# Stick-breaking loop on one core: the order of ScalarE's sigmoids and copies

## The reference

```python
z = einsum('bhtd,bshd->bhts', qb, k) * scale          # scores of a block of 128 queries
mask = s_pos[None, :] < t[:, None]
log_1m = where(mask, log_sigmoid(-z), 0.0)
log_a = log_sigmoid(z) + cumsum(log_1m, axis=3, reverse=True) - log_1m
a = where(mask, exp(log_a), 0.0)
out = einsum('bhts,bshd->bthd', a, v)
```

## Time and profile before

| what | value |
|---|---|
| median of three runs | 2631.31 us (2630.29 to 2631.83) |
| the profiled execution's own time | 2629.57 us |
| its span, first to last instruction | 2627.8 us |
| TensorE busy (all matmuls) | 2556.5 us, 97% |
| VectorE, ScalarE, GpSimd busy | 62%, 45%, 14% |
| the loop of the 40 tiles | about 854 to 945 us of the span |

### The profile page before, as it was taken

One profiled execution on the slowest core, in us unless ns is written; L12 is line 12 of the kernel. 1 busy time (PEld: TensorE's weight loads), 2 busy tenths in 40 slices (PEclk: granted clock), 3 DMA queues, 4 the chain that ended last, 5 costly groups with the idle time before them and its releaser, 6 DMA issues.

```text
span 2627.8 us, 38306 instructions
## 1 busy us (share of the span) xinstructions
PE 2556.5 (97%) x13432; PEld 2156.4 (82%) x13432; DVE 1621.5 (62%) x2801; ACT 1182.2 (45%) x1819; POOL 359.9 (14%) x322
## 2 busy tenths in 40 slices
PE   8999999999999899999999999999999999999997
PEld 6899978888888577888878878888879998788886
DVE  6588667664253647667346667664385885766733
ACT  4367554443232845444235554443343774544421
POOL 1011121110010522111010021110010111211100
PEclk9999999999999999999999999999999999999999
DMA  4410023332233012332322123333233001233231
GB/s 159 137 33 2 25 81 104 96 96 96 83 107 97 9 57 88 97 96 80 112 78 73 33 83 102 96 96 96 87 112 111 17 2 49 82 97 97 93 104 49
DMA packets 61908, 210.91 MB, mean 80 GB/s; under 512 B 8528, under 2 KB 10320, under 8 KB 61776
## 3 DMA queue, kind: packets, MB, share of 16 engines
q1 hardware_dynamic: 61776, 209.13, 25.1%
HBM read 207.01 MB, written 2.10 MB: 80 GB/s over the span
## 4 chain that ended last, share of the span: by engine, by line
PE 90%; DVE 7%; ACT 2%; issue 1%; POOL 0%; DMA 0%; SPq 0%; DVEq 0%; ACTq 0%; POOLq 0%
PE psum L304 21%; PE psum L305 21%; PE psum L306 21%; PE psum L1076 6%; PE psum L1064 3%; PE psum L905 3%; PE psum L907 3%; PE psum L906 3%; PE psum L1054 2%; PE psum L1053 2%; DVE xl L477 2%; DVE h L494 1%; PE psum L338 1%; DVE dh L493 1%; PE psum L332 1%
## 5 line engine op out<-in xcount | busy, mean ns | idle before, releaser
L304 PE MATMUL psum<-xh,w_hi 128*128 128x512 f32 x1712 | 667.0, 390 | 0.1
L305 PE MATMUL psum<-xh,w_lo 128*128 128x512 f32 x1712 | 666.1, 389 | 0.0
L306 PE MATMUL psum<-xl,w_hi 128*128 128x512 f32 x1712 | 666.1, 389 | 0.0
L266 DVE TENSOR_TENSOR w_lo<-w_raw,w_hi 128x1024 fp32r<-128x1024 f32 x226 | 280.2, 1251 | 513.4 <-ACT w_hi L260 511.4
L260 ACT ACTIVATE w_hi<-w_raw 128x1024 fp32r<-128x1024 f32 x226 | 236.1, 1057 | 564.8 <-PE psum L306 455.1
L304 PEld LDWEIGHTS psum<-xh,w_hi 128*128 128x128 f32 x1712 | 321.4, 188 | 66.9 <-issue 0.6
L306 PEld LDWEIGHTS psum<-xl,w_hi 128*128 128x128 f32 x1712 | 321.4, 188 | 66.7
L305 PEld LDWEIGHTS psum<-xh,w_lo 128*128 128x128 f32 x1712 | 321.5, 188 | 66.1
L698 DVE TENSOR_TENSOR w_lo<-w_raw,w_hi 128x1024 fp32r<-128x1024 f32 x160 | 209.3, 1308 | 253.7 <-ACT w_hi L694 253.7
L694 ACT ACTIVATE w_hi<-w_raw 128x1024 fp32r<-128x1024 f32 x160 | 168.4, 1053 | 234.7 <-PE psum L306 234.7
L304 PE MATMUL psum<-ah,w_hi 128*128 (+1 forms) x704 | 273.9, 389 | 0.0
(11 more groups left out here) (197 smaller groups left out, 3849.7 us busy)
## 6 DMA issues: line engine op xcount, KB each, us to landing
w_raw<-w_up SPq DMA_DIRECT2D x176, 512.0 KB, 3.6
w_raw<-w_down SPq DMA_DIRECT2D x88, 512.0 KB, 3.6
w_raw<-nsa_in SPq DMA_DIRECT2D x56, 512.0 KB, 3.8
w_raw<-sb_in SPq DMA_DIRECT2D x24, 512.0 KB, 3.6
w_raw<-nsa_out SPq DMA_DIRECT2D x16, 512.0 KB, 3.6
w_raw<-swa_in SPq DMA_DIRECT2D x10, 512.0 KB, 4.0
w_raw<-sb_out SPq DMA_DIRECT2D x8, 512.0 KB, 3.5
w_raw<-swa_out SPq DMA_DIRECT2D x8, 512.0 KB, 3.6
```

The costliest lines, as they stand in the source:

```text
L266: nc.vector.tensor_tensor(w_lo[:, u % RING, :], w_raw[:, u % RING, :], w_hi[:, u % RING, :].bitcast(F32), ALU.subtract).then_inc(split_don ...
L304: nc.tensor.matmul(bank(p, o), wh[:, k, o, :], xhi(k), start=(first and k == 0), stop=False)
L305: nc.tensor.matmul(bank(p, o), wl[:, k, o, :], xhi(k), start=False, stop=False)
L306: mm = nc.tensor.matmul(bank(p, o), wh[:, k, o, :], xlo(k), start=False, stop=(last and k == 1))
```

## The change

In ScalarE's list the four sigmoid calls of tiles 0 to 3 come first, then `split_hi` and the four value scalings. Its round is then: copy of `s - 4`, copy of `s - 3`, sigmoids of `s`, sigmoids of `s + 1`. The two `output` calls of a group of ten stand after the sigmoids of tile `s` = 14, 24, 34 and the next one, where they stood after the copies of tiles 10 and 11 (20 and 21, 30 and 31). In VectorE's list the `split_lo` stands after scan 3 where it stood after scan 1, and the two `low` calls after scan 15 (25, 35) where they stood after scan 13 (23, 33). The lists of TensorE and GpSimd are the same.

```diff
-            sigmoids(0)
-            sigmoids(1)
+            for s in range(4):
+                sigmoids(s)
             split_hi(act, u0 + 23 + AHEAD)
             values(1)
-            for s in range(2, SB_TILES, 2):
+            for s in range(4, SB_TILES, 2):
+                copy(s - 4)
+                copy(s - 3)
                 sigmoids(s)
-                copy(s - 2)
                 sigmoids(s + 1)
-                copy(s - 1)
-                if s >= 12 and s % 10 == 2:
+                if s >= 14 and s % 10 == 4:
                     output(s // 5 - 2)
                     output(s // 5 - 1)
-            copy(SB_TILES - 2)
-            copy(SB_TILES - 1)
+            for s in range(SB_TILES - 4, SB_TILES):
+                copy(s)
             output(DC - 2)
             output(DC - 1)
...
             for s in range(SB_TILES):
                 sticks(s)
-                if s == 1:
+                if s == 3:
                     split_lo(dve, u0 + 23 + AHEAD)
-                if s >= 13 and s % 10 == 3:
+                if s >= 15 and s % 10 == 5:
+                    low(s // 5 - 3)
                     low(s // 5 - 2)
-                    low(s // 5 - 1)
```

## The result

| | before | changed |
|---|---|---|
| median | 2631.22 us (2630.29 to 2631.83) | 2616.36 us (2615.49 to 2616.97) |
| runs | 5 | 5 |
| profiled execution, its span | 2629.57, 2627.8 us | 2616.5, 2614.7 us |
| loop, first scores to the projection's first product | 853.42 to 944.59: 91.17 us | 853.93 to 931.36: 77.43 us |

The changed kernel is faster: ratio 0.9944, 95% interval 0.9930 to 0.9957. The medians are 14.9 us apart.

What follows compares the result with a forecast made beforehand. A chain through several engines, not a full engine, was taken to set the loop's pace. Gains of 7.9 and 4.3 us, together 12.2, took 2629.57 to 2617.4; plus 1.74 for the median gave 2619.1 us, range 2616.5 to 2624.5.

Steps and rivals of the forecast that it cites:

- (a): Loop rounds: sigmoids no longer wait behind late copies; two-round chain falls from 7.62 us to 6.77, or 7.02 with split tiles.
- (b): Loop start: four sigmoids ahead of the split; sigmoid of tile 14 at 880.5 instead of 888.37, 7.9 us earlier.
- (c): TensorE at the loop's start: the gap and the clock fall go, 1.63 us, counted within (b).
- (d): Outputs, each ten tiles: value products of the pair 10 wait for low; 7.88 us instead of 6.77, 1.1 us three times.
- (e): Whole loop: 7.9 us at the start, 4.3 in twenty tiles, nothing from tile 34; together 12.2 us.
- the median stands 1.74 above it: Step from profiled execution to median: 1.74 us added to 2617.4, giving 2619.1 us.
- a missing output wait: Range's lower end: output wait at nothing, 3 x 1.1 less, of which about 2.5 us passes; 2616.6 us.
- larger output wait: Rival at the outputs: wait of 2.2 us instead of 1.1, three times; 2622.4 us; chance 0.14.
- clock: Rival: TensorE's clock falls in the new loop; once 1.63 us, 2620.7; once every ten tiles 6.5 us, 2625.6; chance 0.06.
- no other round: Rival: round stays at 4.06 us, only start and clock won, some 2.5 us; 2628.8, no change; chance 0.05.
- Slower: Rival: TensorE held at value products of the pair 10 until low; decides from about 5.2 us each; 2635 at 6.5; chance 0.04.

Runs made afterwards that it cites:

- x5: Against the changed kernel: round reordered to copy s-4, sigmoids s, copy s-3, sigmoids s+1, so the copies are no longer adjacent; 2620.91 us.
- x3: Changed kernel with the old start: split and value scalings behind the sigmoids of tile 1, VectorE's split behind scan 1; 2619.88 us.
- x12: Changed kernel with one output between the round's two sigmoids and one behind, low calls behind scans 14 and 15; 2616.38 us.
- x1: The kernel before, unchanged, run again for a second profile; 2630.91 us.
- x9: The kernel before, unchanged, run again for a third profile; 2631.16 us (one run).
- x6: Changed kernel with both low calls one scan later, behind scan 16 (26, 36); 2631.99 us.

## Why the prediction was right or wrong

**(a) The link that goes: right.** A sigmoid no longer waits for a late copy. By x5 the lag and the adjacency of the copies have about equal parts in it (0.49 and 0.42 us from tile 18 to 22); the prediction did not price them apart. The mis-sized term is the second scan of a pair. I put it at 1.26 us behind the first, duration plus a gap. It is 1.14, so the chain has 6.62 us instead of 6.77 with tiles of 512 (tile 20 to 24) and 6.89 instead of 7.02 with split ones (18 to 22).

**(b) and (c) The start and its clock: right.** 26.89 us from the first scores to the sigmoid of tile 14 where 34.95 were; 8.1 us for the 7.9 predicted. (That the sigmoids of 14, 24 and 34 stand at 880.82, 898.53 and 916.23, so near the predicted 880.5, 898.6 and 916.7, is in part luck: the loop began 0.51 us later.) The split cost nothing on the path. The clock stays at 1.00, and x3 prices its fall at 1.47 (1.63 predicted).

**(d) The outputs: right in place and releaser, a little too dear.** 14 to 18 took 7.53 us where I had 7.88. Over the chain of 6.62 it costs 0.91 us, not 1.1. Of the 0.35 us between 7.88 and 7.53, 0.24 lies ahead of the value products of the pair 10, mostly in the two scans (2.34 us together, not 2.5), and 0.11 behind them (the transposes of 14 and 15 take 1.02 us, not 1.16). The wait at the value products is 0.7 us. The prediction had it as the only limit there; x12 shows a second one right beneath it, ScalarE's list with the two outputs in it, at 7.40 us.

**(e) The sum: the step that failed.** It has three parts. The two stretches of ten tiles give 5.16 us instead of 4.3, by (a) and (d). The last stretch, which the sum put at nothing, gives 0.5: from tile 34 to 38 it takes 7.52 us where I had 7.88, and from there to the projection 7.61 where I had 7.75. And "the median stands 1.74 above it" did not hold for both kernels. It stood 1.65 above the profiled execution before, but 0.1 below it after. What I took for a fixed distance was in all likelihood, by x1 and x9, a clock fall at the loop's end that two of three profiled executions of before have and none of the changed kernel's three. The profiled executions are 13.07 us apart: 13.74 in the loop, less 0.51 for its later start and some 0.15 behind it. 1.65 + 0.14 us more are in the medians: 14.86. Against the predicted 12.2 the loop is off by 1.5 us and the step to the medians by 1.8; the later start and the 0.15, which are scatter, take 0.7 of this back, and without that luck the forecast would have missed by more.

The range's lower end was 2616.5: it took in a missing output wait, but neither the chain's error nor a clock fall that the first profile did not show.

Of the rivals, "larger output wait", "clock", "no other round" are excluded by the ten tiles at 17.7 with a clock of 1.00. "Slower" did not happen, and x6 shows how near its place is: one scan.

## What to carry to other kernels

Where no engine is full and a loop still takes longer than each of them needs, follow one item from its step back to the same step of a later item, and look at what stands in the list ahead of it although it is not needed there; let such work lag by a round, and keep it together where it would otherwise stand between two steps that the chain needs. Price links of queued instructions by the distance of their starts, not by the duration of one. And before a profiled execution is subtracted from a median, look for thin stretches of TensorE in it: a clock fall behind them may be in the median and not in the profile.

## What the runs showed of the hardware

After a stretch in which TensorE was busy 0.55 to 0.66 of 2 us, with a wait of 1.45 us, the granted clock of the next 3 us was 1.00 in one execution and 0.55 and 0.56 in two, of the same kernel; the same 32 matmuls took 1.90 or 3.56 us. So whether it falls is not fixed by the program. With a wait of 3.8 us in x6 it was at 0.73, 0.50 and 0.63 over nine microseconds, where 0.50 is 1.2 GHz throughout, and it did so at all three such waits; the expected 9 us came out as 15. The Trainium skill, "TensorE: Matmul & The Clock Gate", "HAM oscillation — how this bites in real kernels", describes such falls behind waits for data; here they came from waits for another engine.

Queued instructions start closer together than their records last: two 128x512 scans take 2.34 us together and start 1.14 us apart, where one alone lasts 1.22.

The trace names as releaser what ended last by its account. For the wait at 885.13 it named a copy (line 1964) that those value products don't need; with `low` moved by one scan it named `low`.
